# Three 256-column matmuls per weight tile, accumulated in one PSUM region, in a two-block transformer kernel

## The reference

```python
proj = u @ w_in[i]                                                  # (256, 2048) @ (2048, n)
h = h + rmsnorm(mixed @ w_out[i], g_mix_post[i])
ff = jnp.square(jax.nn.relu(u2 @ w_up[i])) @ w_down[i]
gate = jax.nn.sigmoid(rmsnorm(h, g_ple_pre[i]) @ w_ple_gate[i])
```

## Time and profile before

| what | value |
|---|---|
| runs | 2942.71, 2973.05, 2975.55 us; median 2973.05 |
| profiled execution, span from first to last instruction | 2975.2 us |
| TensorE matmul busy | 2867.4 us, 96% of the span, 16,001 matmuls |
| TensorE weight load busy | 2470.6 us, 83% |
| VectorE busy | 1954.4 us, 66% |
| ScalarE busy | 1424.9 us, 48% |
| GpSimd busy | 261.1 us, 9% |
| data moved | 510.35 MB, mean 172 GB/s |

### The profile page before, as it was taken

How to read it: one execution, slowest core, us unless ns; L and a number is a source line. 1 busy time by engine, 2 the same in 40 slices (tenths; PEclk the granted TensorE clock), 3 DMA queues, 4 the chain that set the end, 5 groups by cost and what they waited for, 6 DMA issues and landing times.

```text
span 2975.2 us, 43913 instructions
## 1 busy us (share of the span) xinstructions
PE 2867.4 (96%) x16001; PEld 2470.6 (83%) x16001; DVE 1954.4 (66%) x2245; ACT 1424.9 (48%) x1757; POOL 261.1 (9%) x162
## 2 busy tenths in 40 slices
PE   7999999997999999999886999999999999999998
PEld 6888888886888888888775788888888888888887
DVE  6566666667655656566688566766766566656885
ACT  5445454444444444444354455554544444444554
POOL 2000000014000000001234000102100000000210
PEclk9999999998999999999988999999999999999999
DMA  6554545563656665666543355445555555555553
GB/s 213 166 168 161 169 153 190 183 187 110 186 185 188 188 185 179 188 185 189 162 129 108 121 179 171 142 156 179 178 189 185 190 175 192 185 182 192 164 181 127
DMA packets 499726, 510.35 MB, mean 172 GB/s; under 512 B 8586, under 2 KB 496288, under 8 KB 499648
## 3 DMA queue, kind: packets, MB, share of 16 engines
q1 hardware_dynamic: 498576, 508.46, 53.8%
q0 software_dynamic: 1072, 0.83, 0.1%
HBM read 507.16 MB, written 2.10 MB: 171 GB/s over the span
## 4 chain that ended last, share of the span: by engine, by line
PE 89%; DVE 6%; ACT 2%; issue 2%; DMA 0%; POOL 0%; DVEq 0%; SPq 0%; ACTq 0%
PE ps L1622 57%; PE ps L1623 29%; DVE split L1009 2%; DVE X L1040 1%; DVE E L1467 1%; DVE h L1066 1%; ACT split L567 1%; PE pw L1729 1%; PE pw L1711 1%; ACT X L591 0%; DMA raw<-in_w_in 0%; POOL G L437 0%; PE pw L1658 0%; PE pw L1730 0%; PE pw L1724 0%
## 5 line engine op out<-in xcount | busy, mean ns | idle before, releaser
L1622 PE MATMUL ps<-X,split 128*128 128x512 f32 x7168 | 2558.0, 402 | 69.8 <-issue 47.4
L1623 PE MATMUL ps<-X,split 128*128 128x256 f32 x7168 | 2022.7, 282 | 0.0
L1622 PEld LDWEIGHTS ps<-X,split 128*128 128x128 f32 x7168 | 1358.8, 190 | 405.1 <-issue 66.4
L1009 DVE TENSOR_TENSOR split<-raw,split 128x1024 fp32r<-128x1024 f32 x968 | 1200.2, 1263 | 555.4 <-ACT split L567 547.5
L1623 PEld LDWEIGHTS ps<-X,split 128*128 128x128 f32 x7168 | 1366.3, 191 | 0.8
L567 ACT ACTIVATE split<-raw 128x1024 fp32r<-128x1024 f32 x968 | 1008.9, 1055 | 719.2 <-PE ps L1623 714.6
L573 ACT ACTIVATE cross<-ps 128x512 f32<-128x512 f32 x252 | 150.4, 597 | 435.3 <-PE ps L1623 435.2
L1622 PE MATMUL ps<-split,X 128*128 128x512 f32 x512 | 187.2, 408 | 0.0
L1623 PE MATMUL ps<-split,X 128*128 128x256 f32 x512 | 144.8, 283 | 0.0
L1022 DVE TENSOR_TENSOR t<-ps,cross 128x512 f32<-128x512 f32 x90 | 62.3, 692 | 111.2 <-ACT cross L573 111.1
L1622 PEld LDWEIGHTS ps<-split,X 128*128 128x128 f32 x512 | 97.5, 190 | 31.1 <-issue 8.1
(11 more groups left out here) (245 smaller groups left out, 1176.6 us busy)
## 6 DMA issues: line engine op xcount, KB each, us to landing
raw<-in_w_up SPq DMA_DIRECT2D x152, 1024.0 KB, 5.7
raw<-in_w_in SPq DMA_DIRECT2D x136, 1024.0 KB, 5.1
raw<-in_w_down SPq DMA_DIRECT2D x96, 1024.0 KB, 5.5
raw<-in_w_out SPq DMA_DIRECT2D x32, 1024.0 KB, 5.4
raw<-in_w_ple_gate SPq DMA_DIRECT2D x32, 1024.0 KB, 5.4
raw<-in_w_down SPq DMA_DIRECT2D x16, 768.0 KB, 4.6
raw<-in_w_br_moba SPq DMA_DIRECT2D x8, 1024.0 KB, 5.5
raw<-in_w_br_diff SPq DMA_DIRECT2D x8, 1024.0 KB, 5.5
```

The costliest lines, as they stand in the source:

```text
L1009: TT(split[:, k % RING, :, 1, :], raw[:, (k // 2) % RING, HALF * (k % 2):HALF * (k % 2) + HALF, :], split[:, k % RING, :, 0, :], ALU.subtr ...
L1622: MM(ps[:, bank, :], stay_hi, move, start=start, stop=False, skip_group_check=True)
L1623: ins = MM(ps[:, bank, 0:TOK], stay_lo, move[:, 0, :], start=False, stop=stop, skip_group_check=True)
```

## The change

In `blocks` a 128x128 piece of weights now meets three moving operands of 256 columns each: hi weights by activation hi, hi weights by activation lo, lo weights by activation hi. All three accumulate into columns 0 to 255 of the same bank. The tensor `cross`, its copies on ACT, the semaphores `cross_done` and `tiles_done`, and the DVE instruction that added the two regions are gone. DVE reads the sums from PSUM in the instruction that multiplies by the norm, adds to `G` or `h`, or scales the values, and waits for PE's count of halves (`half_used`) in place of ACT's count of copies. Where nothing else was to be done (out1, the first pass of the MLP's down projection, proj) it is a copy. The clearing of `G` on POOL ahead of the first MLP is gone, since the first pass now writes it.

```diff
@@ -174,7 +174,6 @@
     X2 = sb("X2", [P, KT, 2, TOK], F32R)
     G = sb("G", [P, KT, TOK])
     E = sb("E", [P, KT, TOK])
-    cross = sb("cross", [P, 2, 2, TOK])
     t = sb("t", [P, 2, 2, TOK])
     sg = sb("sg", [P, 2, TOK])[:, :, :]
     con = sb("con", [P, NCONST])
...
@@ -257,7 +255,7 @@
     gate_w_landed = sem("gate_w_landed")
     pair_used = sem("pair_used")
     hi_done, lo_done, half_used = sem("hi_done"), sem("lo_done"), sem("half_used")
-    cross_done, evac_done = sem("cross_done"), sem("evac_done")
+    evac_done = sem("evac_done")
     vec_turned, vec_copied = sem("vec_turned"), sem("vec_copied")
     x_turned, eps_ready = sem("x_turned"), sem("eps_ready")
     p_turned, p_hi, p_ready = sem("p_turned"), sem("p_hi"), sem("p_ready")
...
@@ -488,11 +486,9 @@
         scale_g(0, 1)
         fold_squares(1)
 
-        pool.wait_ge(x1_ready, 12)
         pool.wait_ge(sums_done, 3)
-        nc.gpsimd.memset(G[:, :, :], 0.0).then_inc(tiles_done, 1)
         clear_acc()
-        sum_units(7, tiles_done, TILES_FFN1 + 24, g_tile)
+        sum_units(7, evac_done, U0["ffn1"] + 56, g_tile)
         scale_g(1, 3)
         fold_squares(2)
 
...
@@ -566,18 +562,10 @@
                 act.wait_ge(half_used, k - RING + 1 + 8 * at.turn)
             A(split[:, k % RING, :, 0, :], raw[:, (k // 2) % RING, HALF * (k % 2):HALF * (k % 2) + HALF, :], ACT.Copy).then_inc(hi_done, 1)
 
-        def evac(at, m, u):
-
-            s = (at.u + u) % 2
-            act.wait_ge(half_used, at.halves(m) + 1)
-            A(cross[:, s], ps[:, 2 * s:2 * s + 2, TOK:512], ACT.Copy).then_inc(cross_done, 1)
-
         def each_half(at, rows, after, final=False):
-            for m, (u, _, _, _, _, _, last) in enumerate(rows):
+            for m in range(len(rows)):
                 if not (final and m + LEAD >= len(rows)):
                     hi(at, m)
-                if last:
-                    evac(at, m, u)
                 after(m)
 
         def root(k, bank, scale=1.0 / DM):
...
@@ -780,21 +768,8 @@
         loop(act, steps, 3, 0, ffn1, start=1)
         ffn1(3)
 
-        def proj_granule(at, g, k):
-
-            hi(at, 2 * g)
-            for c in range(4):
-                if c < 3:
-                    act.wait_ge(pair_used, 3 * k + c + 1)
-                    s = (at.u + 4 * g + c) % 2
-                    A(cross[:, s], ps[:, 2 * s:2 * s + 2, TOK:512], ACT.Copy).then_inc(cross_done, 1)
-                else:
-                    evac(at, 2 * g + 1, 4 * g + c)
-            hi(at, 2 * g + 1)
-
-        s = At("proj1")
-        proj_granule(s, 0, 0)
-        proj_granule(s, 1, 1)
+        for m in range(4):
+            hi(At("proj1"), m)
         root(3, 0)
         gained_and_square_chunks(2, 3, "g_ple_pre")
 
...
@@ -1009,28 +983,29 @@
             TT(split[:, k % RING, :, 1, :], raw[:, (k // 2) % RING, HALF * (k % 2):HALF * (k % 2) + HALF, :],
                split[:, k % RING, :, 0, :], ALU.subtract).then_inc(lo_done, 1)
 
-        def evac(at, u, dst):
+        def unit_sums(at, u):
 
             s = (at.u + u) % 2
-            dve.wait_ge(cross_done, at.unit(u) + 1)
-            TT(dst, ps[:, 2 * s:2 * s + 2, 0:TOK], cross[:, s], ALU.add).then_inc(evac_done, 1)
-
-        def evac_normed(at, u, dst, norm=rn[:, 1, :]):
-
-            s = (at.u + u) % 2
-            dve.wait_ge(cross_done, at.unit(u) + 1)
-            steps.step(TT(dst, ps[:, 2 * s:2 * s + 2, 0:TOK], cross[:, s], ALU.add))
-            settled()
-            TT(dst, dst, over(norm, 2), ALU.mult).then_inc(evac_done, 1)
-
-        def evac_values(at, u):
-
-            s = (at.u + u) % 2
-            dve.wait_ge(cross_done, at.unit(u) + 1)
-            steps.step(TT(V, ps[:, 2 * s:2 * s + 2, 0:TOK], cross[:, s], ALU.add))
-            settled()
-            steps.step(nc.vector.tensor_scalar(V[:, 0, :], V[:, 0, :], rn_col[:, 0:1], None, ALU.mult))
-            nc.vector.tensor_scalar(V[:, 1, :], V[:, 1, :], rn_col[:, 1:2], None, ALU.mult).then_inc(evac_done, 1)
+            return ps[:, 2 * s:2 * s + 2, 0:TOK]
+
+        def summed(at, u, m):
+
+            dve.wait_ge(half_used, at.halves(m) + 1)
+            return unit_sums(at, u)
+
+        def evac(at, u, m, dst):
+
+            nc.vector.tensor_copy(dst, summed(at, u, m)).then_inc(evac_done, 1)
+
+        def evac_normed(at, u, m, dst, norm=rn[:, 1, :]):
+
+            TT(dst, summed(at, u, m), over(norm, 2), ALU.mult).then_inc(evac_done, 1)
+
+        def evac_values(at, u, m):
+
+            unit = summed(at, u, m)
+            steps.step(nc.vector.tensor_scalar(V[:, 0, :], unit[:, 0, :], rn_col[:, 0:1], None, ALU.mult))
+            nc.vector.tensor_scalar(V[:, 1, :], unit[:, 1, :], rn_col[:, 1:2], None, ALU.mult).then_inc(evac_done, 1)
 
         def gained_lo(e, c, gain):
 
...
@@ -1230,19 +1205,16 @@
                 s0 = (s.u + 3 * n) % 2
                 pair = bass.ds(4 * i + 2 * n, 2)
                 if m % 8 == 3:
-                    evac_normed(s, 3 * n, t[:, s0], mix_rn)
+                    evac_normed(s, 3 * n, m, t[:, s0], mix_rn)
                 if m % 8 == 5:
 
-                    evac(s, 3 * n + 1, t[:, 1 - s0])
-                    evaced(s, 3 * n + 1)
-                    steps.step(TT(G[:, pair, :], G[:, pair, :], t[:, 1 - s0], ALU.mult))
+                    dve.wait_ge(sig_done, 8)
+                    TT(G[:, pair, :], G[:, pair, :], summed(s, 3 * n + 1, m), ALU.mult).then_inc(evac_done, 1)
                 if m % 8 == 7:
 
                     dve.wait_ge(sig_done, 8 + 2 * i + n + 1)
-                    evac(s, 3 * n + 2, t[:, s0])
+                    TT(t[:, s0], summed(s, 3 * n + 2, m), sg, ALU.mult).then_inc(evac_done, 1)
                     evaced(s, 3 * n + 2)
-                    steps.step(TT(t[:, s0], t[:, s0], sg, ALU.mult))
-                    settled()
                     TT(G[:, pair, :], G[:, pair, :], t[:, s0], ALU.add).then_inc(gated, 1)
                     dve.wait_ge(gated, 2 * i + n + 1)
             each_half(s, BRANCH, after)
...
@@ -1311,36 +1283,40 @@
                         embed(0, EMB1)
                     if m % 4 == 3:
                         u = m // 4
-                        tile, pair = t[:, (s.u + u) % 2], bass.ds(4 * i + 2 * u, 2)
-                        evac(s, u, tile)
-                        evaced(s, u)
-
-                        dve.wait_ge(tiles_done, TILES_FFN1 + b * 8 + 2 * i + u)
-                        TT(G[:, pair, :], G[:, pair, :], tile, ALU.add).then_inc(tiles_done, 1)
+                        pair = bass.ds(4 * i + 2 * u, 2)
+                        if first:
+                            evac(s, u, m, G[:, pair, :])
+                        else:
+                            dve.wait_ge(evac_done, s.unit(u))
+                            TT(G[:, pair, :], G[:, pair, :], summed(s, u, m), ALU.add).then_inc(evac_done, 1)
                 each_half(s, DOWN, after)
             if first:
                 up(0)
-            loop(dve, steps, 4, 2, up, start=int(first))
+            loop(dve, steps, 4, 0, up, start=int(first))
             if last:
                 down(0)
             loop(dve, steps, 4, 0, down, start=int(last))
         ffn1(0)
-        loop(dve, steps, 3, 8, ffn1, start=1)
+        loop(dve, steps, 3, 0, ffn1, start=1)
         ffn1(3)
 
-        dve.wait_ge(tiles_done, TILES_FFN1 + 32)
+        dve.wait_ge(evac_done, U0["ffn1"] + 64)
         square_last(G, sq, 1)
 
-        def proj_granule(at, g):
+        def proj_granule(at, g, k):
             lo(at, 2 * g)
             for c in range(4):
                 u = 4 * g + c
-                evac(at, u, E[:, 2 * u:2 * u + 2, :])
+                if c < 3:
+                    dve.wait_ge(pair_used, 3 * k + c + 1)
+                else:
+                    dve.wait_ge(half_used, at.halves(2 * g + 1) + 1)
+                nc.vector.tensor_copy(E[:, 2 * u:2 * u + 2, :], unit_sums(at, u)).then_inc(evac_done, 1)
             lo(at, 2 * g + 1)
 
         s = At("proj1")
-        proj_granule(s, 0)
-        proj_granule(s, 1)
+        proj_granule(s, 0, 0)
+        proj_granule(s, 1, 1)
         inverse_root(3)
         post_norm(1, "g_mlp_post", lo_behind(3, "g_ple_pre"))
         gained_lo(3, 3, "g_ple_pre")
...
@@ -1517,20 +1493,17 @@
                         embed(1, EMB2)
                     if m % 4 == 3:
                         uu = m // 4
-                        tile, pair = t[:, (s.u + uu) % 2], bass.ds(4 * i + 2 * uu, 2)
-                        evac(s, uu, tile)
-                        evaced(s, uu)
-
-                        dve.wait_ge(tiles_done, tiles + 2 * i + uu + outer_tiles)
-                        TT(h[:, pair, :], h[:, pair, :], tile, ALU.add).then_inc(tiles_done, 1)
+                        pair = bass.ds(4 * i + 2 * uu, 2)
+                        dve.wait_ge(evac_done, s.unit(uu))
+                        TT(h[:, pair, :], h[:, pair, :], summed(s, uu, m), ALU.add).then_inc(evac_done, 1)
```

(56 more changed lines are left out.)

45 lines of the change are left out of this document (22 added, 23 removed).

## The result

The changed kernel takes 3009.25 us (median of 4 runs, 3008.1 to 3010.19); the kernel before, with a fourth run beside the three shown, 2959.55 us (2942.71 to 2975.55). The ratio is 1.0167, 95% interval 1.0127 to 1.0207: the changed kernel is slower, by 1.3 to 2.1%. The forecast was 2953, range 2920 to 3010. The time fell just inside the range, on the wrong side of no change.

What follows compares the result with a forecast made beforehand. The prediction took PE, busy 96% of the span, as the bound. From the profiled 2975.2 us it took 6 for the matmul stream and 14 for PE's waits: 2955, with 2953 forecast for the median, range 2920 to 3010.

Steps and rivals of the forecast that it cites:

- What bounds the kernel: Whole kernel: PE sets the time, busy 2867.4 of 2975.2 us; relieving DVE and ACT pays only where PE waits.
- The matmul stream: All 7680 pairs: three 256-column matmuls take 351.5 ns against 352.3 for the pair, -6 us in all.
- twice the short distance minus the long one: Test on PE's start distances for a fixed cost per matmul: 234.3 - 235.1 = -0.8 ns over the whole trace.
- The third weight load: 7680 more loads on PE: each streams in 109 ns, under the 117 of a 256-column matmul, so cost nothing.
- Adding to the same columns: Three matmuls accumulating in the same PSUM columns: no stall, as in the gate projection, cost zero.
- The relief of DVE and ACT does not speed up PE: DVE loses 166 us and ACT 158; no faster matmuls, since 346 against 353 ns a pair was put down to DMA.
- PE's waits: Chains PE waits for, at gate, out1, proj, probabilities, ffn2b and attention: 13.8 us saved, floor 0, ceiling about 20.
- The waits for DVE in the proj stages: PE waits 5.3 us in four places for DVE's evacuations, which come earlier: 4.0 us saved.
- those for the probabilities: PE's transposes of the probabilities wait 2.0 us in four places; DVE's values come 1.3 earlier: all 2.0 saved.
- the fixed cost per matmul: Rival: the first MLP's +6.6 ns per triple holds for all matmuls, +51 us, 3010 us; chance 0.15.
- the load as the bound: Rival, every triple: loads don't keep up with 117 ns; at 125 ns a distance 3133 us; chance 0.10.
- The signs it named: Trace after: triples of 350 to 354 ns in the second MLP; 0.125 us distances prove load or fixed cost; over 8 ns off 352 refutes.

Runs made afterwards that it cites:

- Run 8: On the kernel before, the lo weights too were moved over by 512 columns, so no 256-column matmul was left: 3713.46 us.
- run 2: On the changed kernel, the third matmul was cut in two of 128 columns each, with the same weights loaded twice: 3775.95 us.
- runs 13 and 14: Changed kernel and kernel before, each with 64 of 128 weight columns in all matmuls of three tiles in four: 2906.35 and 2898.99 us.
- run 1: On the kernel before, the 512-column matmul was split into two of 256, copies and extra pass kept: 3024.58 us, ratio 1.0229.
- run 6: On the kernel before, weight loads after the ring's first four blocks brought an eighth of the bytes: 2958.9 us.

## Why the prediction was wrong

- **What bounds the kernel**: right. PE's stream is the time before and after.
- **The matmul stream, -6 us**: wrong. It is +50 us in the timelines, 360.0 against 352.3 ns at full clock. The step that failed is "a fixed cost per matmul would show as twice the short distance minus the long one". In an alternating stream the start of a matmul is shifted against its neighbours, and only the sum of the two distances means something. Run 8 and the changed kernel give each kind among its own, 226.5 and 120.0, and twice the short less the long is then +13.5, not -0.8. The row that warned was the 119.9 of the first MLP. The mean over the whole trace was taken for the fair value, and it mixed the two ends of one uncertain split.
- **The third weight load, nothing**: wrong, and this is the cause as far as the runs show it. 109 ns under 117 said that it fits, and by throughput it nearly does (116 ns a load in run 2). But with 64-column loads the third matmul is free (runs 13 and 14, 340.0 both), and with full ones it costs 6.7 to 13.3 ns. Fitting in the time of one matmul was not enough: neither the load's 116 nor the columns' 113.3 gives the 120.0 of the two together in a row. The gate projection could not show it: its distances are read to 10 ns, it has long and short matmuls, too, and its loads are the narrow ones.
- **Adding to the same columns, nothing**: right (run 1).
- **The relief of DVE and ACT does not speed up PE**: right; the reason given, that DMA makes the 353, was wrong (run 6).
- **PE's waits, -14 us**: right in the sum, -14.2. The waits for DVE in the proj stages gave 2.4 us of the 4.0 put down for them; those for the probabilities gave 3.6, where 2.0 was put down.
- **The rivals**: the fixed cost per matmul, 3010 us at a chance of 0.15, came true in its price and not in its mechanism. It was priced from the 119.9 ns of one stretch, which is what a short matmul costs in a row of its like; but with narrow loads (runs 13 and 14) a matmul costs nothing by itself, so that 3010 came so near is in part luck. The slower rival, the load as the bound, had the right place and the wrong mechanism: its margin of 8 ns did not hold, but not because a load lasts longer than 117 ns. The rule of the Trainium skill (TensorE: Matmul & The Clock Gate, Back-to-back issue gap), 2.5 ns a matmul, would have had the right sign and, with 19 us of 50, under half of the size. That section gives it for the isolated matmul and says that in a stream of loads and matmuls both set the spacing, which agrees with the 120.0 and 113.3 ns here.
- **The signs it named**: a triple of 350 to 354 ns in the second MLP came out as 359.8 and told that it was wrong. The others were set too wide: 120.0 is no "0.125 us or more", and 360.0 is not more than 8 ns from 352.
- **The start**: the forecast set out from a profile of 2975.2 us, in the slow rhythm for some nine tenths of its stream. Where the kernel before was executed more often, its medians were 2958 to 2960. Against the fast rhythm the third matmul costs 13.3 ns, against the slow one 6.7.

Open: how load and matmul hold each other up in a row of short matmuls, whether the width of the load or that of the output does it, why 16-column loads aren't quicker than 64-column ones, and what sets the rhythm of the kernel before.

## What to carry to other kernels

The columns are not all of a matmul's price. At a moving size of 256 in this format, a further matmul with a full 128-column load cost 7 to 13 ns for the same columns. On a kernel bound by PE, 7680 of them cost 50 us, while the 280 us taken off DVE and ACT were nearly all hidden work and gave back 14. Price a split by runs in which one kind of matmul stands alone, not by differences inside an alternating stream; and where PE is the bound, take from the other engines only at the places where PE waits.

## What was not expected of the hardware

- With 64-column loads only columns are paid for: 768 columns take 340.0 ns in two matmuls and in three (0.4427 ns a column, 1/2.4 GHz would be 0.4167). With full 128-column loads a matmul of 512 columns stays at that price (226.5 ns), and one of 256 in a row of its like takes 120.0 ns in place of 113.3.
- Four full loads over 768 columns took 463 ns in run 2, 116 a load, so the loads of its 128-column matmuls weren't hidden.
- The alternation of 512 and 256 columns has two stable rhythms, 353.3 and 346.7 ns, at a DMA share of 0.59 and of 0.08. Grouping equal lengths gave 348 and 349 ns and runs within 0.1%, against 1.1% of scatter before.
